# The order of work in neighbourhood attention, and the opening of a dense feed-forward stage

## The reference, cut to what matters

```python
hl = _modulate(_rmsnorm(xl, norm_g[i, 0]), ml[0], ml[1])
q, k, v = jnp.split(h @ w_qkv, 3, axis=-1)          # 16 heads of 64; q and k are rms-normed
# each latent row attends to an 8 x 16 window (with bias rpb) and to the context
y = softmax(q @ k.T + bias) @ v @ w_o
xl = xl + ml[2] * yl
# dense SwiGLU on the normed, modulated tokens
a, b = jnp.split(h @ w_in, 2, axis=-1)
y = (silu(a) * b) @ w_out
```

## Time and profile before

| | us |
|---|---|
| median of 3 runs (2740.16 to 2744.35) | 2740.83 |
| the profiled execution's own time | 2745.18 |
| its span (first to last instruction) | 2743.2 |
| attention's projection starts, in the span | 52.5 |
| pair 0's step 0 staged | 94.1 |
| dense stage's P1 starts | 613.5 |
| mean granted TensorE clock | 0.977 |

### The profile page before, as it was taken

One profiled execution on the slowest core, in us unless ns is written; L12 is line 12 of the kernel. 1 busy time (PEld: TensorE's weight loads), 2 busy tenths in 40 slices (PEclk: granted clock), 3 DMA queues, 4 the chain that ended last, 5 costly groups with the idle time before them and its releaser, 6 DMA issues. The chain is left out here.

```text
span 2743.2 us, 43707 instructions
## 1 busy us (share of the span) xinstructions
PE 2623.9 (96%) x17527; PEld 1667.9 (61%) x17528; DVE 1010.3 (37%) x2331; ACT 661.4 (24%) x1383; POOL 501.4 (18%) x465
## 2 busy tenths in 40 slices
PE   6999999889999999998999999999997999999997
PEld 3555555455555555555777677767744458668484
DVE  2354445327676764013444444444423111010110
ACT  3344444222221220015313232323202111010110
POOL 0111111013332324321223122312200010000000
PEclk8999999989999999999999999999998999999999
DMA  7224322313333333101111001100209997595831
GB/s 246 68 68 104 98 67 68 103 46 92 107 107 119 109 114 85 43 21 29 27 33 33 24 10 33 32 24 10 71 0 350 344 327 236 169 304 176 258 118 27
DMA packets 321293, 295.03 MB, mean 108 GB/s; under 512 B 5920, under 2 KB 285600, under 8 KB 321024
## 3 DMA queue, kind: packets, MB, share of 16 engines
q1 hardware_dynamic: 315648, 273.17, 33.0%
q0 software_dynamic: 4352, 15.60, 2.3%
q10 hardware_dynamic: 1152, 4.19, 0.4%
HBM read 279.83 MB, written 11.53 MB: 106 GB/s over the span
## 5 line engine op out<-in xcount | busy, mean ns | idle before, releaser
L2351 PE MATMUL bank<-hidden,weight_ring 128*128 128x512 f32 (+1 forms) x768 | 308.7, 536 | 1.8 <-ACT work L2695 1.8
L655 PE MATMUL bank<-weight_ring,hidden 128*128 128x384 f32 x760 | 267.4, 496 | 4.8 <-ACT work L799 4.6
L1283 PE MATMUL bank<-hidden,weight_ring 128*128 128x384 f32 x704 | 238.6, 493 | 4.9 <-ACT hidden L426 4.9
L1429 DVE SCALAR_TENSOR_TENSOR weight_ring<-weight_ring,silu_c 128x256 f32<-128x256 f32 x308 | 213.9, 735 | 5.5
L655 PEld LDWEIGHTS bank<-weight_ring,hidden 128*128 128x128 f32 x760 | 138.1, 191 | 109.1 <-ACT work L799 16.6
L1283 PEld LDWEIGHTS bank<-hidden,weight_ring 128*128 128x128 f32 x704 | 133.2, 192 | 93.7 <-issue 7.0
L2351 PEld LDWEIGHTS bank<-hidden,weight_ring 128*128 128x128 f32 x768 | 134.9, 190 | 82.4 <-issue 68.1
L1283 PE MATMUL bank<-weight_ring 128*128 128x384 f32 x528 | 182.4, 496 | 0.3 <-DVE work L1437 0.3
L1798 PE MATMUL bank<-work,weight_ring 128*128 128x224 f32 x768 | 147.7, 354 | 0.0
L1798 PEld LDWEIGHTS bank<-work,weight_ring 128*128 128x128 f32 x768 | 144.1, 190 | 1.9 <-ACT work L1880 1.6
L1833 PE MATMUL bank<-weight_ring,work 128*128 128x512 f32 x320 | 141.8, 599 | 1.0 <-ACT work L1880 1.0
(11 more groups left out here) (386 smaller groups left out, 3909.8 us busy)
## 6 DMA issues: line engine op xcount, KB each, us to landing
weight_ring<-in_moe_w_in SPq DMA_DIRECT2D x64, 1024.0 KB, 10.1
weight_ring<-in_ada_w SPq DMA_DIRECT2D x38, 1024.0 KB, 5.4
weight_ring<-in_ffn_w_in SPq DMA_DIRECT2D x44, 512.0 KB, 4.9
hidden<-in_moe_w_out SPq DMA_DIRECT2D x8, 2816.0 KB, 9.8
residual<-in_moe_w_out SPq DMA_DIRECT2D x8, 2816.0 KB, 15.0
work<-in_moe_w_in SPq DMA_DIRECT2D x16, 1024.0 KB, 9.6
weight_ring<-in_na_w_qkv SPq DMA_DIRECT2D x24, 512.0 KB, 8.2
weight_ring<-in_gdn_w_qkv SPq DMA_DIRECT2D x24, 512.0 KB, 5.5
```

The source lines that it names most:

```text
L655: mm = nc.tensor.matmul(m.psum[6][:, 0:3 * P], m.H[:, k, t * P:(t + 1) * P], weights(u)[:, k, :], start=(k == 0), stop=(k == KD - 1))
L1283: mm = nc.tensor.matmul(bank[:, 0:HT], w[:, k, :], t[:, k, :], start=(first and k == 0), stop=(last and k == HK - 1), skip_group_check=True)
L1429: nc.vector.scalar_tensor_tensor(out=out, in0=ada_slab[:, k, :], scalar=by, in1=out, op0=ALU.mult, op1=ALU.add).then_inc(acc_ok, 1)
L2351: mm = nc.tensor.matmul(B[b][:, c0:c0 + t1 - t0], W[:, s, k, :], m.H[:, k, t0:t1], start=(k == 0), stop=(k == KD - 1))
```

## The change

1. Pair 0's projection uses the banks 6 and 4 in turn, so that a tile waits for the tile before the last. Flip 0 stands behind tile 4, flip 1 behind tile 5 (before: both behind tile 5).
2. In step 4 half tile 10 and flip 1 come behind the transposes instead of ahead of them, and ScalarE takes the transposed probabilities out ahead of the exponential of step 5 and of flip 1.
3. SyncE issues the two slabs ahead of the weights.
4. Dense stage: the norm's spread uses the banks 6 and 7. P1 waits for its groups one by one. VectorE makes T1 between the scalings of group 5 and 6. T4 goes from VectorE to GpSimd, behind T3.

```diff
-    HALVES = (((0,), (1,), (2,)), ((3,), (4,), (5,)), ((6,), (7,), ()), ((8,), (9,), ()), ((10,), (), ()), ((), (11,), ()))
+    HALVES = (((0,), (1,), (2,)), ((3,), (4,), (5,)), ((6,), (7,), ()), ((8,), (9,), ()), ((), (10,), ()), ((), (11,), ()))
...
                     load_attention_bias(m, sp, pair + 1)
-                if not isinstance(i, int):
-
-                    sp.wait_ge(projected, pair * 6 + 6)
-                    load_attention_weights(m, sp, u, pair + 2)
-                else:
...
                 for j in range(ADA_SLABS):
                     s, _, _, before = ada_steps[u * ADA_SLABS + j]
                     sp.wait_ge(ada_used, i * (2 * ADA_SLABS) + before)
                     col = pair * (WIN * ADA_SLABS) + (2 * D + WIN * j)
                     sp.dma_start(ada_slab(s), adaw[0][:, :, bass.ds(col, WIN)]).then_inc(ada_in[s], 16)
+                if not isinstance(i, int):
+
+                    sp.wait_ge(projected, pair * 6 + 6)
+                    load_attention_weights(m, sp, u, pair + 2)
+                else:
+
+                    sp.wait_ge(projected, pair * 6 + 6)
+                    for g in ((4, 5, 6) if u else (0, 1, 2)):
+                        load_output_weights(m, sp, g)
...
             for t in range(6):
-                for n in (2 * t, 2 * t + 1):
-                    if n:
-                        half_tile(n, 0, 0)
-                    else:
-                        for k in range(4):
-                            nc.tensor.matmul(m.psum[6][:, 0:3 * P], m.H[:, k, 0:P], weights(0)[:, k, :], start=(k == 0), stop=False)
-            for g in range(2):
-                flip(g, 0)
+                if t >= 2:
+                    pe.wait_ge(v_out, t - 1)
+                for k in range(KD):
+                    mm = nc.tensor.matmul(m.psum[FIRST_BANKS[t % 2]][:, 0:3 * P], m.H[:, k, t * P:(t + 1) * P], weights(0)[:, k, :],
+                                          start=(k == 0), stop=(k == KD - 1))
+                mm.then_inc(projected, 1)
+                if t >= 4:
+                    flip(t - 4, 0)
...
-                    if n == 4 and more:
-                        flip(1, pair + 1)
...
                     halves(n, 1)
+                    if n == 4 and more:
+                        flip(1, pair + 1)
...
             for t in range(6):
-                take_raw(t, 0, 0)
+                take_raw(t, 0, 0, FIRST_BANKS[t % 2])
                 if t in (3, 5):
                     take_root(t // 4, 0)
-            for g in range(2):
-                take_flipped(g, 0, 0)
+                if t >= 4:
+                    take_flipped(t - 4, 0, 0)
...
+                    if n == 4:
+                        take_turned(n, pair)
                     if n + 1 < N or more:
                         exp(n + 1, pair)
...
+                    if n != 4:
+                        take_turned(n, pair)
...
+            pool.wait_ge(tokens_ok, 2)
+            nc.gpsimd.tensor_tensor(T4, m.H[:, HK:KD, 0:HT], T2, ALU.subtract).then_inc(tokens_ok, 1)
             body(0, 1)
...
                         for k in range(HK):
+                            if as_ready:
+                                pe.wait_ge(*pre.ready(k))
...
-                    pe.wait_ge(*pre.ready(HK - 1))
-                    multiply(x, raw(c, 0, 0), m.H[:, 0:HK, 0:HT], last=False)
+                    multiply(x, raw(c, 0, 0), m.H[:, 0:HK, 0:HT], last=False, as_ready=True)
...
-            pre.on_vector(dve)
-            dve.wait_ge(*pre.ready(HK - 1))
-            nc.vector.tensor_tensor(T1, m.H[:, 0:HK, hi], m.H[:, 0:HK, lo], ALU.subtract).then_inc(tokens_ok, 1)
+            def first_sum():
+                dve.wait_ge(*pre.ready(HK - 1))
+                nc.vector.tensor_tensor(T1, m.H[:, 0:HK, hi], m.H[:, 0:HK, lo], ALU.subtract).then_inc(tokens_ok, 1)
+            pre.on_vector(dve, between=(KD - 2, first_sum))
...
-            dve.wait_ge(tokens_ok, 2)
-            nc.vector.tensor_tensor(T4, m.H[:, HK:KD, lo], T2, ALU.subtract).then_inc(tokens_ok, 1)
...
-        swiglu(m, Norm(m, 0, 1), ahead=swiglu_ahead(m))
+        swiglu(m, Norm(m, 0, 1, banks=(6, 7)), ahead=swiglu_ahead(m))
```

More of the change, by code:

```diff
@@ L384, with __init__ @@
 class Norm:
-    def __init__(self, m, layer, norm):
-        self.m, self.layer, self.norm = m, layer, norm
+    def __init__(self, m, layer, norm, banks=(1, 2)):
+        self.m, self.layer, self.norm, self.banks = m, layer, norm, banks
         self.base = m.norm_base
@@ L411, in on_tensor @@
             for t in range(t0 // P, t1 // P):
-                mm = nc.tensor.matmul(m.psum[1 + b][:, t * P - t0:(t + 1) * P - t0], self.rs[:, t:t + 1].to_broadcast([P, P]), const(m, C_IDENT),
+                mm = nc.tensor.matmul(m.psum[self.banks[b]][:, t * P - t0:(t + 1) * P - t0], self.rs[:, t:t + 1].to_broadcast([P, P]), const(m, C_IDENT),
                                       start=True, stop=True)
@@ L427, in on_scalar, with on_vector @@
                                      scale=m.MODA[:, self.layer, self.norm, k, v:v + 1]).then_inc(hidden, 1)
-    def on_vector(self, dve):
+    def on_vector(self, dve, between=(KD, None)):
         m, nc = self.m, self.m.nc
@@ L435, in on_vector @@
         for k in range(KD):
+            if k == between[0]:
+                between[1]()
             for b, (t0, t1, _) in enumerate(self.parts):
                 dve.wait_ge(spread, self.base[3] + b + 1)
-                nc.vector.tensor_tensor(m.H[:, k, t0:t1], m.X[:, k, t0:t1], m.psum[1 + b][:, 0:t1 - t0], ALU.mult).then_inc(scaled, 1)
+                nc.vector.tensor_tensor(m.H[:, k, t0:t1], m.X[:, k, t0:t1], m.psum[self.banks[b]][:, 0:t1 - t0], ALU.mult).then_inc(scaled, 1)
 def attention_weights(m, u):
@@ L576, in body @@
                     load_attention_bias(m, sp, pair + 1)
+                for j in range(ADA_SLABS):
+                    s, _, _, before = ada_steps[u * ADA_SLABS + j]
+                    sp.wait_ge(ada_used, i * (2 * ADA_SLABS) + before)
+                    col = pair * (WIN * ADA_SLABS) + (2 * D + WIN * j)
+                    sp.dma_start(ada_slab(s), adaw[0][:, :, bass.ds(col, WIN)]).then_inc(ada_in[s], 16)
                 if not isinstance(i, int):
@@ L585, in body @@
                         load_output_weights(m, sp, g)
[L586 to L590, removed]
                 if not more:
@@ L793, in _, with take_raw @@
             e64 = const(m, C_EPS + 1, 1)
-            def take_raw(t, pair, u):
+            def take_raw(t, pair, u, bank=6):
                 act.wait_ge(projected, pair * 6 + (t + 1))
-                nc.scalar.copy(raw(t), m.psum[6][:, 0:2 * P]).then_inc(raw_out, 1)
-                nc.scalar.copy(v[:, u, t, :], m.psum[6][:, 2 * P:3 * P]).then_inc(v_out, 1)
+                nc.scalar.copy(raw(t), m.psum[bank][:, 0:2 * P]).then_inc(raw_out, 1)
+                nc.scalar.copy(v[:, u, t, :], m.psum[bank][:, 2 * P:3 * P]).then_inc(v_out, 1)
             def take_root(batch, pair):
@@ L818, in exp, with take_turned @@
                                          bias=stats[:, b:b + 1], accum_out=stats[:, b + 2:b + 3]).then_inc(exped, 1)
+            def take_turned(n, pair):
+                for h in range(2):
+                    act.wait_ge(turned, (pair * N + n) * 2 + h + 1)
+                    act.wait_ge(weighted, pair * N + n + N)
+                    nc.scalar.copy(PT[:, h, 0:cols(n)], m.psum[2 + h][:, 0:cols(n)]).then_inc(turned_out, 1)
             act.wait_ge(qk_gain, 2)
             for t in range(6):
-                take_raw(t, 0, 0)
+                take_raw(t, 0, 0, FIRST_BANKS[t % 2])
                 if t in (3, 5):
                     take_root(t // 4, 0)
-            for g in range(2):
-                take_flipped(g, 0, 0)
+                if t >= 4:
+                    take_flipped(t - 4, 0, 0)
             exp(0, 0)
@@ L1279, in _, with multiply @@
                     x, y, z = B[3 * c], B[3 * c + 1], B[3 * c + 2]
-                    def multiply(bank, w, t, first=True, last=True):
+                    def multiply(bank, w, t, first=True, last=True, as_ready=False):
                         for k in range(HK):
+                            if as_ready:
+                                pe.wait_ge(*pre.ready(k))
                             mm = nc.tensor.matmul(bank[:, 0:HT], w[:, k, :], t[:, k, :], start=(first and k == 0), stop=(last and k == HK - 1),
```

1 line of the change is left out of this document (added).

## The result

The changed kernel takes 0.9896 of the time of the one before, 95% interval 0.9884 to 0.9909: 28.5 us less (25 to 32), by medians 2714.21 against 2742.59 in the same set. Run again later on another chip it had 0.9892 (0.9877 to 0.9907). The prediction was 2712 for a kernel before of 2740.83, or 28.7 less. All ratios leave out slow executions: one of 11975 us of the kernel before, beside the first four experiments, and one of 3393 us of the version with T3 and T4 on VectorE.

What follows compares the result with a forecast made beforehand. TensorE, busy 96% of the span, was taken as the bound. Terms 4.9 + 6.5 + 8.6 + 10.5 - 1.8 = 28.7 us less, from a median of 2740.83 to 2712; range 2703 to 2723.

Steps and rivals of the forecast that it cites:

- pair 0's projection: Attention, pair 0: two banks and earlier flip 0 shorten the tiles' waits and the staging of step 0; 4.9 us less.
- slabs, pairs 1 to 6: Attention, modulation product L693: slabs issued ahead of the weights end its waits in these pairs; 6.5 us less.
- step 4, seven pairs: Attention, value product L784: half tile 10 and flip 1 cover the copies it waits for; 10.5 us less.
- pair 7: Attention, step 1: slabs in time and 2.4 GHz bring the value product earlier; 8.6 us less, 4.7 if clock stays low.
- dense opening: Dense stage: P1's early start gains nothing, T4 on GpSimd holds VectorE's 16 instructions; 1.8 us more.
- ScalarE's table load and exponential slide behind the copies and still just fit: Step 5: 1.0 to 1.1 us later, fits by 0.4; rival that it comes too late loses 10.5, 2723, chance 0.10.
- the predicted 15.1: Attention: us gained by earlier slabs; rival that slabs are still late loses it, 2727, chance 0.06.
- The rival that the opening gains: Dense stage: VectorE's 16 get through between T3 and T4, L1310 starts 4.2 us earlier; 37.2 less, 2704, chance 0.12.

Runs made afterwards that it cites:

- the first four experiments: Kernel before with one part only: slabs ahead of weights, 0.9953; pair 0's projection, 0.9984; step 4, 0.9966; dense part, 1.0014.
- the last version: Changed kernel with T3 and T4 on VectorE behind T2 and chunk 1's weight sums held back; 0.9861 and again 0.9868 of the kernel before.

## Why the prediction was right

| step | predicted | measured by the ledger |
|---|---|---|
| pair 0's projection | 4.9 | 4.95 |
| slabs, pairs 1 to 6 | 6.5 | 7.2 |
| step 4, seven pairs | 10.5 | 10.4 |
| pair 7 | 8.6 | 8.8 |
| dense opening | -1.8 | -1.55 |
| nothing stated | 0 | +0.7, -0.6, +0.2 |

The prediction took its rows from the same execution of the kernel before that this ledger starts from, so part of the close agreement is built in. The mechanisms rest on the experiments; the sizes of the slabs' terms are one execution's.

- **Projection.** The saving a tile and the end of the chain, VectorE's scaling instead of the scores, came as said. From the projection's start to the staging of step 0 it is 41.6 to 42.4 us in the five kernels with the old projection and 36.4 to 37.6 in the nine with the new one, so this term holds beyond one execution. The 0.7 up to pair 0's slab product are the scores' second group (1.04 us instead of 1.23) and the first half tile (4.16 instead of 4.69), which I had left out.
- **Step 4** is read between the slab products of pair 0 and 1: 7.16 - 5.68 = 1.48 a pair, 10.4 in seven. What is left of 23.32 - 5.68 is the slabs' 7.2. That ScalarE's table load and exponential slide behind the copies and still just fit was the step that could have failed.
- **Slabs.** The queue's order was the cause, shown both ways: alone it removes all of the waits, and with it undone they are back. The size was one execution's: the sum of these waits went from 8.6 to 13.7 in five executions, and the whole cost of the late slabs from 13.2 to 19.4, so that the predicted 15.1 could have been 2 too high or 4 too low by the execution alone: that it met 16.0 is partly luck. One reading was too general. The 5.4 us from issue to landing are the median of all 38 such transfers of the program; the 16 in attention took 7.7 to 10.1 before (median 9.2) and 5.4 to 11.4 after. Pair 7's first slab did land 5.4 after its issue, its second 7.8. The sum of the four parts run alone, 12.9 + 4.4 + 9.3 - 3.8 = 22.8, is below the 28.5 of the whole; each has an interval of 2.3 to 3.6 on either side, and the sum one of about 6, so that the parts add isn't contradicted, nor shown closer.
- **Pair 7.** The half of the gain that is the clock was predicted from the rate at which work behind the wait ran, and measured in two kernels: 5.2 us from transposes to value product. But 4.1 us for the clock is the most that was seen: in the other four executions with late slabs, 12.7 to 13.7 us less 5.2 and less the waits leaves 2.8 to 3.1.
- **Dense opening.** The rival that the opening gains is refuted, by the part alone and by T4 put back. The loss is in the predicted place, of the predicted parts (1.5 for T4 and 0.3 from ScalarE's chain; measured 1.2 and 0.3), and for the predicted reason: GpSimd's T4 and sums and VectorE's instructions exclude each other. The Trainium skill's rule ("SBUF — State Buffer", "Who interferes with whom": an exclusive lock) agrees with L1442's 6.96 us for 0.61 and with the 14 instructions' 10.17 for 6.38.
- The 0.6 us that went between pair 7 and the norm's spread lie in the norm's sums on TensorE (L406): the same 24 records took 4.42 us before and 5.25 after. In all fourteen traces they take 2.81 to 5.25, and both of these values belong to the last version's two executions, so that is the execution and not the change. It stays open why the dense part alone cost 3.8 by runs (1.4 to 6.3) where its trace shows 1.6 in the opening.

## What to carry to other kernels

Where TensorE is the bound, look for short waits that recur in every pass and ask what stands ahead of the late thing in its queue: a transfer needed in this pass behind one needed in the next, or a copy behind work that could come later. A change of order can need both engines' orders at once: TensorE's alone was a loss here. A wait can cost more than its own length where the clock falls in it, by 2.8 to 4.1 us here for 4.7 to 5.6 of waits. Before work is moved from VectorE to GpSimd to relieve it, see in a trace whether VectorE's next instructions are held by GpSimd's. Here both kinds were, `tensor_scalar` and `scalar_tensor_tensor`; then the move lengthens VectorE's line by the slower engine's time, and leaving GpSimd idle was faster.

## What the runs showed that I had not expected

- With the slabs first, the pairs' slab products are 52.27 to 52.28 us apart in the changed kernel, pair after pair; with the weights first, the first ones are 52.4 to 54.1 us apart within one execution of the kernel with SyncE's order undone.
- While GpSimd works without a pause, VectorE gets in exactly one instruction between two of GpSimd's: two instructions against T3 and T4 in 6.96 us, and four of the 14 against the four weight sums (1.37 to 1.48 us each, the other ten some 0.46), which cost 10.17 - 6.38 = 3.8 us, 0.95 each.
- The time of the opening is the same to 0.1 us in all kernels with the same opening (30.3 in five, 31.8 in five), while TensorE's wait in it is 4.2 to 5.1, or 4.6 to 6.3. In the kernel with SyncE's order undone it was 4.6, and P6's 8 records ahead of it took 4.53 us instead of the changed kernel's 2.84: what TensorE loses there, the wait takes up.
